# Key mask rows by a transfer, the last tile's mix behind the fourth head, and the modulation rows in six pieces

## The reference

```python
mod = jax.nn.silu(c) @ w_ada + b_ada
sh_a, sc_a, gt_a, sh_m, sc_m, gt_m = jnp.split(mod[:, None, :], 6, axis=-1)
h = rms_norm(x, g_norm_mix) * (1 + sc_a) + sh_a
proj = h @ w_in                                   # q latent, kv latent, rotary key, g_u, g_v
q = mla_queries(q_lat, q_pos)                     # 8 heads of 96
k, v = mla_keys_values(ckv_all, krope_all, k_pos) # v: 8 heads of 64
mask = (k_pos[None, :] // 64) <= (q_pos[:, None] // 64)
att = softmax(where(mask, q @ k.T * 96 ** -0.5, -inf)) @ v
u, v_rows = gelu(g_u), layer_norm(gelu(g_v), g_ln_v, b_ln_v)
gm = u * (w_spatial_masked @ v_rows + b_spatial)  # in chunks of 128 positions
merged = concatenate([rms_norm(att, g_out_attn), rms_norm(gm, g_out_gmlp)])
x = x + gt_a * (merged @ w_out)
h = rms_norm(x, g_norm_ffn) * (1 + sc_m) + sh_m
x = x + gt_m * hier_moe(h)                        # 32 experts, 2 for each token
```

## Time and profile before

| what | value |
|---|---|
| median of 3 runs | 1185.55 us (1181.13 to 1185.98) |
| profiled execution | 1179.94 us, its span 1178.2 us |
| TensorE busy | 1080.4 us (92%) |
| VectorE, GpSimd, ScalarE busy | 646.3, 317.5 and 271.8 us |
| projection stage | 0 to about 309 us |
| attention heads | about 309 to 750 us |
| experts | about 750 to 1178 us |

### The profile page before, as it was taken

One profiled execution on the slowest core, in us unless ns is written; L12 is line 12 of the kernel. 1 busy time (PEld: TensorE's weight loads), 2 busy tenths in 40 slices (PEclk: granted clock), 3 DMA queues, 4 the chain that ended last, 5 costly groups with the idle time before them and its releaser, 6 DMA issues.

```text
span 1178.2 us, 14254 instructions
## 1 busy us (share of the span) xinstructions
PE 1080.4 (92%) x4836; PEld 700.5 (59%) x4836; DVE 646.3 (55%) x1274; ACT 271.8 (23%) x606; POOL 317.5 (27%) x351
## 2 busy tenths in 40 slices
PE   3599999999967988998999999889999999999993
PEld 0234555555535445666666666777777777777771
DVE  2445555555565366657657577727665544445452
ACT  1132223222322222123222331211111111111110
POOL 1122222222430011111011000114444454544443
PEclk9799999999958799999999999789999999999997
DMA  9973333343430034223213026648989999898940
GB/s 307 337 298 115 137 137 141 147 144 119 167 98 30 33 108 151 90 81 135 90 63 120 16 108 241 266 159 334 337 337 334 338 356 351 334 350 340 352 176 16
DMA packets 78037, 229.55 MB, mean 195 GB/s; under 512 B 29827, under 2 KB 33558, under 8 KB 62230
## 3 DMA queue, kind: packets, MB, share of 16 engines
q1 hardware_dynamic: 50544, 198.63, 45.0%
q0 software_dynamic: 24048, 26.81, 6.7%
q10 hardware_dynamic: 3382, 3.32, 0.8%
HBM read 201.23 MB, written 88.25 MB: 246 GB/s over the span
## 4 chain that ended last, share of the span: by engine, by line
PE 77%; DVE 12%; issue 3%; ACT 3%; DMA 2%; POOL 2%; ACTq 1%; DVEq 0%; POOLq 0%; SPq 0%
PE bank L1005 15%; PE bank L1358 10%; PE bank L1360 10%; PE bank L1375 9%; PE bank L959 9%; PE bank L1172 7%; PE bank L1118 5%; PE bank L1143 4%; PE bank L1090 2%; PE bank L987 2%; DVE probT L2119 1%; PE bank L1016 1%; PE bank L971 1%; DMA grope<-in_g_knorm 1%; ACT qT L1571 1%
## 5 line engine op out<-in xcount | busy, mean ns | idle before, releaser
L1005 PE MATMUL bank<-W_in,hT 128*128 128x512 f32 (+3 forms) x432 | 181.9, 575 | 3.0 <-ACTq L1497 3.0
L806 POOL TENSOR_SCALAR st<-st 128x1 f32<-128x1 f32 (+5 forms) x76 | 17.5, 230 | 591.9 <-DVEq L1716 591.9
L1005 PEld LDWEIGHTS bank<-W_in,hT 128*128 128x128 f32 (+1 forms) x432 | 79.4, 186 | 96.0 <-issue 90.7
L1375 PE MATMUL bank<-WD,hidT 128*128 128x512 f32 x264 | 120.6, 600 | 2.9 <-DVE hidT L2334 2.9
L1358 PE MATMUL bank<-WG,xT 128*128 128x256 f32 x528 | 121.6, 384 | 1.0 <-DVE xT L2318 1.0
L1172 PE MATMUL bank<-W_out,mT 128*128 128x512 f32 (+1 forms) x256 | 122.3, 606 | 0.0
L1360 PE MATMUL bank<-WU,xT 128*128 128x256 f32 x528 | 119.3, 379 | 0.0
L1360 PEld LDWEIGHTS bank<-WU,xT 128*128 128x128 f32 x528 | 100.3, 190 | 13.6
L1358 PEld LDWEIGHTS bank<-WG,xT 128*128 128x128 f32 x528 | 99.2, 193 | 13.8 <-issue 1.4
L2119 DVE COPY probT<-bank 128x512 f32<-128x512 f32 (+3 forms) x104 | 57.0, 548 | 66.2 <-PE bank L959 58.5
L1143 PEld LDWEIGHTS bank<-vall,probT 128*128 128x128 f32 (+1 forms) x656 | 79.9, 191 | 20.8 <-issue 18.4
(11 more groups left out here) (320 smaller groups left out, 1469.9 us busy)
## 6 DMA issues: line engine op xcount, KB each, us to landing
WG<-in_w_gate_e SPq DMA_DIRECT2D x33, 1024.0 KB
WU<-in_w_up_e SPq DMA_DIRECT2D x33, 1024.0 KB
WD<-in_w_down_e SPq DMA_DIRECT2D x33, 1024.0 KB
ada_w<-in_w_ada SPq DMA_DIRECT2D x24, 1024.0 KB, 7.4
residual_scratch<-x_att SPq DMA_DIRECT2D x32, 512.0 KB, 4.4
kbuf<-k_scratch SPq DMA_DIRECT2D x12, 384.0 KB, 5.0
xbuf<-in_x_prompt SPq DMA_DIRECT2D x8, 512.0 KB, 3.5
W_in<-in_w_in SPq DMA_DIRECT2D x2, 2048.0 KB, 19.0
```

The costliest lines, as they stand in the source:

```text
L1005: ins = mm(ps[:R, 0:n], hT[:, place_of[t] % 2, k, :R], W_in[:, k, c0:c0 + n], start=(k == 0), stop=(k == KD - 1))
L1375: ins = mm(psum[5 + half][:], hidT[:, k, :], WD[u][:, k, half * 512:(half + 1) * 512], start=(k == 0), stop=(k == 1))
```

## The change

Three edits. The mask rows of heads 1 to 7 are written by a transfer in SyncE's queue, from the rows of head 0, instead of GpSimd's copy. VectorE's part of the last tile's mix goes behind head 3 of the sample, and its end (the wait for the root and the scaling) behind head 4. The modulation rows are made two banks at a time: the sample's three pairs beside heads 1, 2 and 4, the prompt's beside heads 6 and 7 of the sample and head 1 of the first prompt tile.

```diff
@@ the plan of the heads' side work
+    VECTORS = {(0, 1): (0, 0), (0, 2): (0, 1), (0, 4): (0, 2), (0, 6): (1, 0), (0, 7): (1, 1), (1, 1): (1, 2)}
     def beside(s, h):
         work = []
-        if s == 0 and h in (6, 7):
-            work += [("vectors", h - 6, 0)]
+        if (s, h) in VECTORS:
+            work += [("vectors", *VECTORS[s, h])]
...
         if work == "vectors":
-            return [(("bc", s, j), 1) for j in range(6)]
+            return [(("bc", s, j), 1) for j in (2 * part, 2 * part + 1)]
@@ SyncE
         new_keys(0)
         store_kv(sp, END)
         store_q(LAST)
+        sp.wait_ge(s_kmask, 1)
+        sp.dma_start(kT[QK:KM, 1:H, :], bcast(kT[QK:KM, 0:1, :], [NT, H - 1, SEQ])).then_inc(s_kmask, 16)
         stored_keys(sp, key_order)
@@ GpSimd
         do(g.affine_select(out=kT[QK:KM, 0, :], in_=kT[QK:KM, 0, :], compare_op=ALU.is_ge, fill=0.0, base=P - 1, pattern=[[-1, SEQ]], channel_multiplier=P))
+        g.sem_inc(s_kmask, 1)
         rstd(st[:P, 41:42], st[:P, 41:42])
-        g.wait_ge(s_rs, n_roots)
-        do(g.tensor_copy(kT[QK:KM, 1:H, :], bcast(kT[QK:KM, 0:1, :], [NT, H - 1, SEQ])))
-        g.sem_inc(s_kmask, 1)
@@ TensorE
                 if s == 1:
-                    pe.wait_ge(s_kmask, 1)
+                    pe.wait_ge(s_kmask, 17)
...
-        def rows_of_vectors(s):
-            for j in range(6):
-                which, half = j // 2, j % 2
+        def rows_of_vectors(s, which):
+            for half in range(2):
+                j = 2 * which + half
                 ps = b2.claim(pe, ("bc", s, j))
@@ VectorE
-        def rstd(n=[0]):
+        def rstd(n=[0], signalled=False):
             n[0] += 1
-            dve.sem_inc(s_ms, 1)
+            if not signalled:
+                dve.sem_inc(s_ms, 1)
             dve.wait_ge(s_rs, n[0])
...
             do(V.tensor_tensor_reduce(u_sb[:R, i % 2], gm[:R], gm[:R], 1.0 / GW, 0.0, ALU.mult, ALU.add, st[:R, 41:42]))
-            rstd()
+            if i == LAST:
+                signal(s_ms)
+            else:
+                rstd()
+                mix_scale(R)
+
+        def mix_scale(R):
             do(V.tensor_scalar(gm[:R], gm[:R], st[:R, 41:42], None, ALU.mult))
             signal(s_gm)
+
+        def mix_end():
+            rstd(signalled=True)
+            mix_scale(P)
...
-        def rows_of_vectors(s):
-            if s:
+        def rows_of_vectors(s, which):
+            if s and which == 0:
                 stored_keys(dve, key_order)
                 dve.wait_ge(s_out1["q"], 16 * len(seq))
                 dve.wait_ge(s_out1["gm"], 16 * len(seq))
                 for par in range(2):
                     dve.wait_ge(s_out1[f"lat{par}"], 32 * len(range(par, len(seq), 2)))
-            for j in range(6):
+            for j in (2 * which, 2 * which + 1):
                 ps = b2.read(dve, ("bc", s, j))
...
         row_max(0, 0)
         row_max(0, 1)
-        mix(LAST)
         for s in range(len(seq)):
             for h in range(H):
                 PT(s, h)
...
                 for job in beside(s, h):
                     work(*job)
+                if s == 0 and h == 3:
+                    mix(LAST)
+                if s == 0 and h == 4:
+                    mix_end()
```

More of the change, by code:

```diff
@@ L1297, in rows_of_vectors @@
                 b2.full(ins, ("bc", s, j))
-        work_of = {"prep": lambda s, i: prep(s), "vectors": lambda s, i: rows_of_vectors(s), "mT": lambda s, i: mT_(s),
+        work_of = {"prep": lambda s, i: prep(s), "vectors": rows_of_vectors, "mT": lambda s, i: mT_(s),
                    "W_out": out_, "h2T": lambda s, i: h2T_(s), "router": lambda s, i: router(s), "fold": lambda s, i: fold(),
@@ L2156, in work @@
             if name == "vectors":
-                rows_of_vectors(of)
+                rows_of_vectors(of, part)
             if name == "mT":
```

## The result

The changed kernel takes 1174.49 us (median of 15 runs, 1167.3 to 1181.36), the kernel before 1184.02 us beside it (15 runs, 1178.41 to 1186.52). The ratio, which goes by the means, is 0.9934, 95% interval 0.9911 to 0.9956: 7.8 us faster (the medians alone lie 9.5 apart). A second set of 11 runs gave 0.9932 (0.9909 to 0.9956). Forecast were 1175.5 us and a gain of 10.0 us.

The account below looks back on a forecast made before the run. TensorE, busy 92% of 1178.2 us, was taken as the bound, losing time only when idle or at low clock. Terms summed to 7.7 us, plus 2.3 for the clock: 1185.55 - 10.0 = 1175.5 us, range 1167 to 1182.

Parts of the forecast that it names:

- Idle time removed, +8.3: Before the sample's first heads: TensorE no longer waits for VectorE's mix of the last tile, 8.3 us gained.
- Three pieces in the heads, -5.9: Sample heads 1, 2 and 4: eight transposes each, 1.97 us at the low clock, paid in full, 5.9 us lost.
- the clock, +2.3: Sample heads: the clock comes up behind the added transposes and is lost again, 2.3 us gained; chance 0.44.
- the upper bound of 4.5: Sample heads 2 and 4: at full clock each would gain 2.3 us, at most 4.5 together.
- The mix in heads 3 and 4, -0.3: Sample heads 3 and 4: VectorE's slack takes most of the moved mix, 0.3 us lost.
- Heads 6 and 7, +7.2: Sample heads 6 and 7: relieved of most modulation-row banks, they save 3.4 and 3.8 us, 7.2 together.
- The sixth piece, -1.6: First prompt tile, head 1: the fold waits for its copies, 5.9 us after the last sample head instead of 4.28.
- The mask rows and the queue, 0: SyncE's queue: mask transfer lands before its need 34 us after issue, delayed stores and loads have slack; no cost.
- the bounds of 2 and 16: Mask transfer's duration: 2 us from the store of gm, 16 us from W_out's rate on one engine.
- Carried to the end: Behind the router fold: every instruction is the same, so the gain at the fold should last to the end.
- the rival of another low stretch: First prompt tile or later: one more low-clock stretch costs 5 us, giving 1180.5; chance 0.15, with other half-returns of the gain.
- One of the prediction's own signs of being wrong: The forecast is wrong if the fold comes 10 us early and the last tile's heads don't.

Follow-up runs that it names:

- mask rows and mix: Changed kernel with the modulation rows put back as twelve banks at sample heads 6 and 7; ratio to the kernel before 0.9943.
- the mask rows alone: Changed kernel with the mix put back ahead of the heads and the modulation rows at heads 6 and 7; ratio to the kernel before 0.9935, again 0.9939.
- the pieces alone: Changed kernel with GpSimd's mask copy back and the mix ahead of the heads, modulation rows still split; ratio to the kernel before 0.9961.
- the filled kernel before: Kernel before with 44 unread transposes in TensorE's 8.3 us pause; ratio to the kernel before 1.0000, median 1182.04 us.

## Why the prediction came out

*Idle time removed, +8.3.* Right, to the row: no pause over 0.4 us between 328.9 and 344. But the first scores came 1.2 us later behind the first key transposes (11.1 instead of 9.9), since the clock fell earlier; that was in no term, and it left 7.1 us of the 8.3.

*Three pieces in the heads, -5.9, and the clock, +2.3.* The mechanism was right: the clock came up behind the first piece and was lost again. The size was less than half of what it measured. Heads 1 to 5 and the way to head 6 took 25.8 us (330.96 to 356.80); my layout at the low clock had 30.6, so the clock gave 4.8 net of what the mix cost, past the upper bound of 4.5. Head 1 took 6.0 (6.1 laid out) and head 2 3.8 (6.1 low, 3.8 full). Without pieces, and without a pause, the clock stayed low for 23 us, which the kernel with mask rows and mix shows. The Trainium skill, "TensorE: Matmul & The Clock Gate", section What's actually happening, would have had it rise there; this chip's rows do not agree.

*The mix in heads 3 and 4, -0.3.* Mis-sized. VectorE's slack of 2 us was that of a head of 4.1 us. At the full clock head 3 is 2.6 us, the cover is gone, and TensorE waits 1.92 us for head 4's copy; the clock is low from 347 to 350 behind it, in which the piece took 1.97 us instead of 1.09. With the outputs, 1.49 instead of 0.93, that is 3.4 us, paid out of the clock's gain, which was some 8 us before it.

*Heads 6 and 7, +7.2.* 4.15 and 2.93 us for 7.2 and 6.8 before: 7.0.

*The sixth piece, -1.6.* 6.57 us from the last sample head to the fold instead of 4.28: -2.3. Its second bank was waited for 3.29 us, and the pause was followed by the low clock from 371 on.

*The mask rows and the queue, 0.* Right. The transfer took 7.0 us, between the bounds of 2 and 16. The estimate of 6 us from the Trainium skill, "SBUF — State Buffer", section Door 1: The DMA port swizzle, was 1 us short of it. The store of gm came 2.4 us and the reload behind it 1.8 us ahead of what I had laid out, and nobody waited for them.

*Carried to the end.* This is the step that failed in part. A gained 10.55 us, or 11.5 against the middle one of three profiles of before. B lost: 344.8 instead of 340.5 or 343.7. All of its instructions are the same; three short stretches of low clock (412, 460 and 545) that the first profile of before did not have make the difference to it, as the rival of another low stretch had it, only with three. The other two profiles of before have such stretches as well and a B of 343.7; the 1.1 us that are left against them are a longer low stretch at the fold (9.1 us of it within B, 6.8 in the other two). In all fourteen profiles B less half of its time at the low clock is 333.4 to 333.7 us, so nothing but the clock moved it. One of the prediction's own signs of being wrong was thus met in part: the fold came 11.1 us early and the end of B 6.9.

Along A the sum came out partly by errors that cancel: 7.1 for 8.3 up to head 1, -1.3 for -3.9 in heads 1 to 5, 7.0 for 7.2 and -2.3 for -1.6, together 10.5 for 10.0. The time itself, 1174.49 against 1175.5, is nearer than the gain, and that is luck: the base of 1185.55, a median of three, was 1.5 us above the median of fifteen.

The timed gain, 7.8, is 2.2 less than forecast and well inside the range. What stays open is how the gain divides among the edits. In the profiles the mask rows take 6 us off A and mix and pieces 5 more; in the timed runs the mask rows alone bring 7.2 to 7.7 and the whole 7.8 to 8.0, with an interval of some 3 us to either side of each, and the pieces alone bring 4.6. That the executions differ in where the clock falls is shown. The split of the timed runs points to a mix whose pause is gone and whose gain the clock takes back; it is not clear of the noise.

## What to carry to other kernels

Where a granted clock of one half coincides with a stage that looks bound by TensorE, ask first what the clock does to each term: the slack of the other engines there is slack at the low clock only, and work that is moved into it becomes a pause once the clock is full. A pause of TensorE costs more than its length if the clock falls behind it; unread transposes in pauses of 1.4 to 3.3 us were worth 8 us here, as much as the whole change. Before a difference of a few us between two profiles is put down to an edit, profile the old kernel again (three executions of it were 6.5 us apart), and look where the profiled execution stands among the timed runs: that of the filled kernel before was the second fastest of twelve and showed a gain that the runs as a whole did not have.

## What the runs showed of the hardware

- VectorE's scaling of 128x512 elements took 6.48 us beside GpSimd's copy of 8x7168 and 0.49 us without it. The Trainium skill, "SBUF — State Buffer", section Terms, calls the port pair that the two engines share an exclusive lock that is held for a whole instruction; that fits.
- 23 us of TensorE work without a pause (heads of the sample, 64 rows) left the clock at 0.50; in the changed kernel, behind the first pair of banks of 128x128 transposes beside the same work, it stood at 1.00. Behind 44 such transposes in the pause of the kernel before it stood at 1.00 too.
- A transfer within SBUF of 8 partitions of 28 KB, 229 KB, landed in 7.0 us, its issue of 0.9 us included.
- The clock fell within the fold, 16 matmuls of 36 columns, although the pause of 3.3 us ahead of it had been filled up to 0.7 us. It did not always fall behind pauses of 1.2 to 1.4 us: the changed kernel lost it at three of them, and the first profile of before at none of the same three.
